# Seven products for eight (Strassen's scheme) in four of the eleven blocks of each down projection

## What is computed

```python
D_MODEL, SEQ, DEPTH = 1024, 256, 2
D_FF = 2816

def hybrid_layer(x, ...):
    h = rms_norm(x, g_attn_pre)
    ...                       # projection, two kinds of attention, w_out
    x = x + rms_norm(jnp.einsum('bse,ed->bsd', mix, w_out), g_attn_post)
    h = rms_norm(x, g_ffn_pre)
    f = jax.nn.silu(jnp.einsum('bsd,df->bsf', h, w_gate)) * jnp.einsum('bsd,df->bsf', h, w_up)
    x = x + rms_norm(jnp.einsum('bsf,fd->bsd', f, w_down), g_ffn_post)
    return x
```

## Time and profile before

| | |
|---|---|
| time, median of 3 runs | 571.66 us (571.55 to 571.73) |
| span of the profiled execution | 569.7 us |
| PE busy | 562.0 us (99%), 3395 matmuls |
| DVE busy | 375.1 us (66%) |
| ACT busy | 294.0 us (52%) |
| POOL busy | 229.1 us (40%) |

### The profile page before, as it was taken

One profiled execution on the slowest core, in us unless ns is written; L12 is line 12 of the kernel. 1 busy time (PEld: TensorE's weight loads), 2 busy tenths in 40 slices (PEclk: granted clock), 3 DMA queues, 4 the chain that ended last, 5 costly groups with the idle time before them and its releaser, 6 DMA issues.

```text
span 569.7 us, 8885 instructions
## 1 busy us (share of the span) xinstructions
PE 562.0 (99%) x3395; PEld 462.1 (81%) x3395; DVE 375.1 (66%) x487; ACT 294.0 (52%) x420; POOL 229.1 (40%) x451
## 2 busy tenths in 40 slices
PE   8999999999999999999999999999999999999996
PEld 5878878888888888888888878888888888888884
DVE  5799895946755746365597987775855746734622
ACT  6576684664445353263546748574645354425420
POOL 1101001507797797860120000033296797785000
PEclk9999999999999999999999999999999999999999
DMA  8954624538556461478266443525575455352701
GB/s 299 370 210 156 237 89 173 223 133 315 184 217 202 167 221 33 189 294 298 89 239 208 158 167 124 211 76 221 222 258 201 173 217 183 113 221 88 282 1 74
DMA packets 18730, 107.34 MB, mean 188 GB/s; under 512 B 2816, under 2 KB 3072, under 8 KB 7168
## 3 DMA queue, kind: packets, MB, share of 16 engines
q1 hardware_dynamic: 18688, 106.78, 50.8%
HBM read 105.72 MB, written 1.05 MB: 187 GB/s over the span
## 4 chain that ended last, share of the span: by engine, by line
PE 93%; DVE 3%; DMA 1%; ACT 1%; issue 1%; POOL 0%; SPq 0%; DVEq 0%; POOLq 0%
PE bank L1209 84%; PE bank L1249 4%; PE bank L1234 2%; PE bank L1275 2%; PE bank L1302 2%; DVE w_l L812 1%; DMA raw<-in_w_blocks 1%; ACT work L631 0%; DVE work L896 0%; DVE work L874 0%; DVE work L897 0%; DVE work L952 0%; DVE work L902 0%; DVE x L986 0%; ACT work L608 0%
## 5 line engine op out<-in xcount | busy, mean ns | idle before, releaser
L812 DVE TENSOR_TENSOR w_l<-raw,w_h 128x2048 fp32r<-128x2048 f32 x90 | 206.6, 2301 | 112.6 <-ACT w_h L559 112.4
L559 ACT ACTIVATE w_h<-raw 128x2048 fp32r<-128x2048 f32 x90 | 171.7, 1915 | 108.5 <-PE bank L1209 91.5
L1209 PE MATMUL bank<-w_h,actT_h 128*128 128x512 f32 (+1 forms) x568 | 223.9, 394 | 0.1
L517 POOL COPY work<-work 32x128 f32<-32x128 f32 (+1 forms) x384 | 191.3, 498 | 75.6 <-DVE work L1013 59.8
L1209 PE MATMUL bank<-w_h,actT_l 128*128 128x512 f32 (+1 forms) x568 | 219.9, 387 | 0.0
L1209 PE MATMUL bank<-w_l,actT_h 128*128 128x512 f32 (+1 forms) x568 | 219.4, 386 | 0.0
L1209 PEld LDWEIGHTS bank<-w_h,actT_h 128*128 128x128 f32 x568 | 106.8, 188 | 23.1 <-issue 2.5
L1209 PEld LDWEIGHTS bank<-w_h,actT_l 128*128 128x128 f32 x568 | 106.7, 188 | 22.1
L1209 PEld LDWEIGHTS bank<-w_l,actT_h 128*128 128x128 f32 x568 | 106.9, 188 | 20.1
L504 POOL TENSOR_TENSOR norms<-norms,constants 128x1 f32<-128x1 f32 x8 | 2.7, 342 | 131.7 <-ACT bank L658 131.7
L1209 PE MATMUL bank<-w_h,fT_h 128*128 128x512 f32 x160 | 49.4, 390 | 0.0
(11 more groups left out here) (78 smaller groups left out, 396.1 us busy)
## 6 DMA issues: line engine op xcount, KB each, us to landing
raw<-in_w_blocks SPq DMA_DIRECT2D x90, 1024.0 KB, 4.8
bias<-in_b_in SPq DMA_DIRECT2D x8, 256.0 KB, 6.1
raw<-in_w_blocks SPq DMA_DIRECT2D x4, 256.0 KB, 5.9
raw<-in_w_blocks SPq DMA_DIRECT2D x2, 512.0 KB, 8.6
x<-in_x SPq DMA_DIRECT2D x2, 512.0 KB, 10.7
gain_b<-in_g_attn_post SPq DMA_DIRECT2D x2, 512.0 KB, 7.3
bias<-in_g_ffn_pre SPq DMA_DIRECT2D x2, 512.0 KB, 7.4
gain_b<-in_g_ffn_post SPq DMA_DIRECT2D x2, 512.0 KB, 6.5
```

The lines of the kernel that those rows point to most:

```text
L517: ins = nc.gpsimd.tensor_copy(crossed[t][32 * j:32 * j + 32, i * n:(i + 1) * n], squares[t][32 * i:32 * i + 32, j * n:(j + 1) * n])
L559: nc.scalar.activation(w["h"][:, slot(b), :], raw[:, r, :], ACT.Copy).then_inc(hi_ready, 1)
L812: nc.vector.tensor_tensor(w["l"][:, slot(b), :], raw[:, slot(b, RAW), :], w["h"][:, slot(b), :].bitcast(F32), ALU.subtract).then_inc(lo_re ...
L1209: ins = nc.tensor.matmul(bank[BANK_OF[name]][:, 0:n], left[s][:, at + k, tokens(t)], right[r][:, k, c * BANK:c * BANK + n], start=first an ...
```

## The change

Four of the eleven down blocks of each layer are multiplied by Strassen's scheme in Winograd's form. Such a block holds 2 k; with 2 tiles of tokens and 2 halves of the columns it is a product of a 2x2 by a 2x2 matrix of squares. Instead of 8 products of squares (24 matmuls) PE does 7 (21 matmuls). The products use four sums of squares of f (S1 to S4) and four sums of squares of weights (T1 to T4).

- **Blocks.** A fast block is two entries of `BLOCKS`: "raw", the loaded squares (three of its four squares, 1536 columns, are split into high and low, 9 matmuls), and "sum", T1 to T4 (2048 columns, 12 matmuls), which is not loaded. The list is 35 down, 36 raw, 37 sum, 38 down, 39 raw, 40 sum, 41 down, 42 raw, 43 sum, 44 raw, 45 sum, then 46 to 49 down. The number of loads stays 46 a layer. Slots go round by four without a skip.
- **Sums of weights.** `add_squares(n)` on DVE: three `tensor_tensor` from SBUF to SBUF, of 1024, 512 and 512 elements on 128 partitions, each waiting for the one before. ACT's `hi` of a sum block waits for `sums_ready`. A raw block's place in `raw` is free only after its `lo` and its sums.
- **Sums of f.** In chunks 1 and 2 `add_s` on DVE (four `tensor_tensor` of 256 elements) makes S1 to S4 of chunks 0 and 1; `hi_s` on ACT and `lo_s` on DVE (1024 elements each) split them. `add_s` waits for both exchanges of the chunk and stands ahead of `lo_f` and `swiglu`. POOL's exchange waits for it.
- **Joining.** The first product M1 gathers in bank 4, M6, M5 and M7 in banks 5 to 7 over all four fast blocks. ACT copies M1 out (`keep_m1`); DVE adds the combinations to the four result banks (`join_first`, `join_second`, eight operations on 512 columns). PE waits for the joins (`joined`).
- **Order on PE at the end.** After the last fast block: half of block 46 for t = 1, then blocks 46 to 49 for t = 0, then the rest for t = 1.

The core of the diff:

```diff
-KF_OWN = 20
-BLOCKS += [("down", k, 2, 0, D) for k in range(0, KF, 2)]
+FAST = 4
+FAST_CHUNKS = FAST // 2
+RAW_AT = []
+for n in range(FAST):
+    if n < FAST - 1:
+        BLOCKS += [("down", 2 * (FAST + n), 2, 0, D)]
+    RAW_AT += [len(BLOCKS)]
+    BLOCKS += [("raw", 2 * n, 2, 0, D), ("sum", 2 * n, 2, 0, D)]
+FIRST_LATE = len(BLOCKS)
+BLOCKS += [("down", k, 2, 0, D) for k in range(4 * FAST - 2, KF, 2)]
...
+SUMS = 2
+def slot(L, b):
+    return (L * NB + b) % SLOTS
+def before(b):
+    return b - SLOTS
...
+        sums = [gains[:].rearrange("p (a n) -> p a n", a=2), work_row[:, 0:4 * BANK].rearrange("p (a n) -> p a n", a=2)]
+        m1_sum = rope_tmp
+        u4, u2, u3, u7 = (work[:, q, :] for q in (0, 2, 3, 2))
+        s_raw = work_row[:, 0:2 * BANK].rearrange("p (s k n) -> p s k n", s=4, k=2)
...
+                    past_L, past = divmod(load_count(L, b) - RAW, NL)
+                    place_free(lo_ready, past_L * NB + LOADED[past] + 1)
+                    if BLOCKS[LOADED[past]][0] == "raw":
+                        place_free(sums_ready, sums_done(past_L, BLOCKS[LOADED[past]][1] // 2))
...
+                if 0 < c <= FAST_CHUNKS:
+                    pool.wait_ge(s_added, FAST_CHUNKS * L + c)
...
+                if m == "sum":
+                    act.wait_ge(sums_ready, sums_done(L, k0 // 2))
...
+            def hi_s(L, c):
+                act.wait_ge(s_added, FAST_CHUNKS * L + c + 1)
+                nc.scalar.activation(s_tiles("h", c), s_raw.rearrange("p s k n -> p (s k) n"), ACT.Copy
+                                     ).then_inc(s_hi_ready, 1)
+            def keep_m1(L):
+                act.wait_ge(block_used, USED.done(L, FIRST_LATE - 2) + USED.n)
+                nc.scalar.activation(m1_sum, products[0][:], ACT.Copy).then_inc(m1_kept, 1)
...
+                        if c <= FAST_CHUNKS:
+                            hi_s(L, c - 1)
                         after(L, b + 3)
                 hi_f(L, FFN_CHUNKS - 2, 0)
+                after(L, FIRST_DOWN)
                 hi_f(L, FFN_CHUNKS - 2, 1)
-                for b in range(FIRST_DOWN, NB - 4):
+                for b in range(FIRST_DOWN + 1, NB - 4):
+                    if b == RAW_AT[FAST - 1]:
+                        keep_m1(L)
                     after(L, b)
-                    if b == FIRST_DOWN + 4:
+                    if b == RAW_AT[1]:
                         hi_f(L, FFN_CHUNKS - 1, 0)
                         hi_f(L, FFN_CHUNKS - 1, 1)
...
+            def add_s(L, c):
+                for t in range(T):
+                    dve.wait_ge(crossed_in[t], f_count(L, c))
+                if L or c:
+                    dve.wait_ge(s_lo_ready, FAST_CHUNKS * L + c)
+                s1, s3, s2, s4 = (s_raw[:, q].rearrange("p k (i b) -> p k i b", b=32) for q in range(4))
+                a11, a12 = f_odd(c, 0, 0), f_odd(c, 0, 1)
+                a21, a22 = f_odd(c, 1, 0), f_odd(c, 1, 1)
+                nc.vector.tensor_tensor(s3, a11, a21, ALU.subtract)
+                link(L, nc.vector.tensor_tensor(s1, a21, a22, ALU.add))
+                link(L, nc.vector.tensor_tensor(s2, s1, a11, ALU.subtract))
+                nc.vector.tensor_tensor(s4, a12, s2, ALU.subtract).then_inc(s_added, 1)
+            def lo_s(L, c):
+                dve.wait_ge(s_hi_ready, FAST_CHUNKS * L + c + 1)
+                nc.vector.tensor_tensor(s_tiles("l", c), s_raw.rearrange("p s k n -> p (s k) n"),
+                                        s_tiles("h", c).bitcast(F32), ALU.subtract).then_inc(s_lo_ready, 1)
...
+            def add_squares(L, n):
+                b = RAW_AT[n]
+                r = raw_slot(L, b)
+                dst = sums_of(n)
+                b12, b11, b22, b21 = (raw[:, r, q * BANK:(q + 1) * BANK] for q in range(4))
+                dve.wait_ge(raw_in[r], raw_done(L, b))
+                link(L, nc.vector.tensor_tensor(dst[:, 0, :].rearrange("p (a n) -> p a n", a=2),
+                                                raw[:, r, BANK:3 * BANK].rearrange("p (a n) -> p a n", a=2),
+                                                b12.unsqueeze(1).broadcast_to([P, 2, BANK]), ALU.subtract))
+                link(L, nc.vector.tensor_tensor(dst[:, 1, 0:BANK], dst[:, 0, BANK:2 * BANK], b11, ALU.add))
+                nc.vector.tensor_tensor(dst[:, 1, BANK:2 * BANK], b21, dst[:, 1, 0:BANK], ALU.subtract
+                                        ).then_inc(sums_ready, 1)
+            def join(L, t, c, what):
+                x = bank[BANK_OF["down", t, c]]
+                nc.vector.tensor_tensor(x[:], x[:], what, ALU.add).then_inc(joined, 1)
+            def join_first(L):
+                _, m6, m5, _ = products
+                dve.wait_ge(m1_kept, L + 1)
+                join(L, 0, 0, m1_sum)
+                dve.wait_ge(products_full, 3 * L + 1)
+                link(L, nc.vector.tensor_tensor(u2, m1_sum, m6[:], ALU.add))
+                dve.wait_ge(products_full, 3 * L + 2)
+                link(L, nc.vector.tensor_tensor(u4, u2, m5[:], ALU.subtract))
+                join(L, 0, 1, u4)
+            def join_second(L):
+                _, _, m5, m7 = products
+                dve.wait_ge(products_full, 3 * L + 3)
+                link(L, nc.vector.tensor_tensor(u3, u2, m7[:], ALU.add))
+                dve.wait_ge(second_begun, L + 1)
+                join(L, 1, 0, u3)
+                link(L, nc.vector.tensor_tensor(u7, u3, m5[:], ALU.subtract))
+                join(L, 1, 1, u7)
...
+                    if c == FFN_CHUNKS - 1:
+                        add_squares(L, 0)
                     after(L, b)
                     for q in range(b + 1, end):
                         after(L, q)
                     if c < FFN_CHUNKS - 1:
+                        if c <= FAST_CHUNKS:
+                            add_s(L, c - 1)
                         lo_f(L, c - 1, 0)
                         lo_f(L, c - 1, 1)
                     swiglu(L, c, 0)
                     after(L, end)
                     if c < FFN_CHUNKS - 1:
                         squares_f(L, c, 1)
-                for t in range(T):
-                    lo_f(L, FFN_CHUNKS - 2, t)
-                    squares_f(L, FFN_CHUNKS - 1, t)
-                for b in range(FIRST_DOWN, NB - 4):
-                    after(L, b)
-                    if b == FIRST_DOWN + 4:
-                        lo_f(L, FFN_CHUNKS - 1, 0)
-                        lo_f(L, FFN_CHUNKS - 1, 1)
+                    if c <= FAST_CHUNKS:
+                        lo_s(L, c - 1)
+                first, second, third, fourth = RAW_AT
+                add_squares(L, 1)
+                lo_f(L, FFN_CHUNKS - 2, 0)
+                squares_f(L, FFN_CHUNKS - 1, 0)
+                after(L, FIRST_DOWN)
+                lo_f(L, FFN_CHUNKS - 2, 1)
+                squares_f(L, FFN_CHUNKS - 1, 1)
+                after(L, first)
+                add_squares(L, 2)
+                after(L, first + 1)
+                after(L, first + 2)
+                after(L, second)
+                add_squares(L, 3)
+                lo_f(L, FFN_CHUNKS - 1, 0)
+                lo_f(L, FFN_CHUNKS - 1, 1)
+                after(L, second + 1)
+                after(L, second + 2)
+                after(L, third)
+                after(L, third + 1)
+                join_first(L)
+                after(L, fourth)
+                after(L, fourth + 1)
+                join_second(L)
...
+                pe.wait_ge(f_lo_ready, F_PARTS.done(L, (c, 1)))
+                pe.wait_ge(s_lo_ready, FAST_CHUNKS * L + c + 1)
+                pe.wait_ge(lo_ready, L * NB + b + 1)
+                product(m1, a11, b11, first, last)
+                product(x12, s4, b22, False, last)
+                product(x11, a12, b21, False, last).then_inc(block_used, 1)
+                USED.tick(b)
+                pe.wait_ge(lo_ready, L * NB + b + 2)
+                ends = [product(m6, s2, t2, first, last), product(m5, s1, t1, first, last),
+                        product(m7, s3, t3, first, last)]
+                if last:
+                    for ins in ends:
+                        ins.then_inc(products_full, 1)
+                product(x21, a22, t4, False, last).then_inc(block_used, 1)
+                USED.tick(b + 1)
...
+                f_landed(L, FFN_CHUNKS - 3, T - 1)
+                for n in range(FAST):
+                    if n < FAST - 1:
+                        multiply(L, 0, RAW_AT[n] - 1)
+                        multiply(L, 1, RAW_AT[n] - 1)
+                    squares(L, n)
+                multiply(L, 1, FIRST_LATE, (0,), asks=True).then_inc(second_begun, 1)
+                multiply(L, 0, FIRST_LATE, asks=False, apart=True)
+                f_landed(L, FFN_CHUNKS - 2, 0)
+                multiply(L, 0, FIRST_LATE + 1)
+                multiply(L, 0, FIRST_LATE + 2)
+                f_landed(L, FFN_CHUNKS - 1, 0)
+                multiply(L, 0, FIRST_LATE + 3)
+                pe.wait_ge(joined, 4 * L + 4)
```

(8 more changed lines are left out.)

189 lines of the change are left out of this document (120 added, 69 removed).

## The result

The changed kernel takes 598.18 us (median of 4 runs, 597.66 to 598.63), the kernel before 571.68 us beside it. The ratio is 1.0465, 95% interval 1.045 to 1.0479: slower, by 26.5 us. The forecast was 595.4 us. A few executions on record were far longer than the others of their kernel (627 us and more); no ratio here uses them.

A forecast was written before the change was run, and what follows sets the result against it. PE, busy 99% at 0.2267 us a matmul, was taken to bound the kernel. Stalls from late DVE and POOL work, less the matmuls saved, came to +12.9 + 10.9 = +23.7 us on 571.66: 595.4 us, range 582 to 604.

The forecast's parts named there:

- X: End of POOL's exchange of chunk 3: later by 3.8 us in each layer, through DVE's sums of f.
- PE's start of the down projection: PE begins at X + 13.15: 233.3 instead of 226.01, and 509.6 instead of 504.20.
- next layer's first blocks: Start of the next layer: its first blocks take their slots as early as before, so nothing is added.
- The first wait: Start of the down projection: PE waits for `swiglu(5, 0)` behind sums, `hi` 37 and `lo` 37; 7.3 and 5.4 us.
- The second wait: Later down blocks: PE waits 1.3 us for `lo` 41 and 4.5 us at block 44, whose `hi` stands behind POOL's copies.
- The joins: End of the down projection: PE waits for the first two joins, 1.15 + 0.9 us a layer.
- The clock falls: Rival: PE's pauses drop it to 1.2 GHz, delaying blocks 44 to 47 by 2 to 4 us a layer; 601 us, chance 0.13.
- Only the handover: Rival: the sums don't hold POOL up, or it catches up while PE stands; 583.0 us, chance 0.16.
- The gain shows: Rival: `swiglu(5, 0)` and every `lo` in time, only saved matmuls and joins count; 566.2, up to 570.3 us, chance 0.08.
- the 0.5 us of air: Before the first down matmul: `swiglu(5, 0)` ends 0.5 us before PE starts, and 2.7 us of sums go in there.

The follow-up runs named there:

- e9: The kernel before with three DVE operations of the weight sums' sizes, results unused, added ahead of `lo` 37: 573.75 us.
- e5: The changed kernel with the sums of weights cut to 8 elements per operation: 585.1 us.
- e6: The changed kernel with the sums of f cut to 8 elements and their low part to one column: 588.44 us.
- e8: The changed kernel with 26 matmuls of 512 columns added on PE ahead of each down projection, to keep it busy through the first wait: 598.11 us.
- e4: The changed kernel with the three additions of `add_squares` replaced by transposes of the same sizes, with one input: 587.99 us.
- e7: The changed kernel with both the sums of weights and the sums of f cut down: 574.47 us.
- e10: The changed kernel with the sums of weights, the sums of f and the joins all cut down: 572.4 us.
- v2: v1 with `keep_m1` and the joins moved ahead of chunk 5's `hi_f` and `lo_f`: 569.62 us, ratio 0.9965 to the kernel before.
- e1: The changed kernel with both Silu moved ahead of `hi` 37 on ACT and both `swiglu` of chunk 5 ahead of `add_squares(0)` on DVE: 598.73 us.
- v1: The changed kernel with two fast blocks instead of four, behind three plain ones, `swiglu(5, 0)` ahead of the last plain `lo`: 588.17 us.

## Why the prediction was right

It was right by its mechanism and its sum. Single terms were off, and part of the closeness of the sum is luck: one term was 3.0 us too small, and the waits behind the start were 1.1 us a layer too large.

| step | predicted, L0 / L1 | measured, L0 / L1 |
|---|---|---|
| X, end of chunk 3's exchange | +3.8 / +3.8 | +4.2 / +6.8 |
| PE's start of the down projection | +7.3 / +5.4 | +7.7 / +8.3 |
| waits and slow matmuls from there to the end of the down projection | 8.3 / 8.3 | 7.15 / 7.15 |
| next layer's first blocks | 0 | 1.05 |
| the layer's part of the loss | +12.9 / +10.9 | +13.4 / +12.8 |

(X is 201.30 + 19.30 and 493.45 + 19.35; the values of layer 1 are less the 13.38 us by which its feed-forward part begins later. The third line is the sum of all distances between matmuls less 0.2267 each. The forecast named 7.85 us of waits there; its own reckoning, from X + 13.15 to X + 69.0, holds 8.3. The fifth is of the profiled spans, 26.1 us together where 23.7 were forecast.)

**X in layer 1 is the term that was mis-sized.** I took POOL's delay as the same addition in both layers. But the kernel before ran in step with PE in layer 1 and not in layer 0, and the change puts both layers out of step, so layer 1 pays the 2 to 3 us that layer 0 had paid already. e9, which found layer 0 in step as well, shows that the course is no property of the layer. These 3.0 us are more than the forecast lacked in all (2.8 us); the waits behind the start, forecast 1.1 us a layer too long, take 2.3 us off again, and the 1.05 us at the next layer's first blocks, which it put at nothing, come on top.

**The first wait** is as described: sums, `hi` 37, `lo` 37, `swiglu(5, 0)`. e5 (6.12) and e6 (3.39) show what the sums of weights and those of f have in it, 2 and 4.7 us in layer 0; 3.5 us had been forecast for what stands without POOL's delay.

**The second wait** was forecast as 1.3 us at block 41 and 4.5 at block 44. The first is in e8 alone (0.93 us); in the changed kernel the slow matmuls ahead of it covered it. The second was 3.42 and 2.75, shorter because `lo` 44 came at X + 48.8 and not at 49.5 and PE came later. Its cause holds: ACT's row waits for POOL, and `hi` 44 stands behind it.

```profile
265.74 0.42 ACT L676 ACTIVATE actT_h<-work 128x256 fp32r<-128x256 f32 x1 [4.96 <-POOL work L590]
266.06 1.47 ACT L641 ACTIVATE w_h<-raw 128x1536 fp32r<-128x1536 f32 x1
```

X + 45.8 was 266.0 by the forecast; the row is at 265.74. In e4, where only the hold on POOL is taken away, this wait is gone. The Trainium skill (SBUF — State Buffer, "Who interferes with whom") gives the contention that the forecast named; e4 agrees for the sums, 41.72 us against 34.71.

**The joins** were forecast at 2.05 us a layer, and show 1.0 and 0.2. In layer 0 `join_first` began at X + 55.4 and not at 56.45; in layer 1 it was as early, and PE came later besides, by the slow matmuls behind the wait at block 44. e7 less e10 puts them at 2.1 us altogether where nothing else is in the way.

**The rivals.** "The clock falls" came half true. The forecast had the matmul stay at 0.2267 us; behind both first waits, and in layer 1 behind block 44 too, matmuls were 0.43 us apart. By e8 the fall after the first wait cost nothing, for the reason given there (PE waits again). The fall behind block 44 in layer 1 made matmuls 1.5 us longer. No run removes it alone, but the third line of the table is 7.15 us in layer 0, without this fall, and in layer 1, with it: what it cost was taken off the waits around it. The Trainium skill (TensorE: Matmul & The Clock Gate, Part 1) has it that an idle PE drops to 1.2 GHz, and the trace agrees after the pauses of 8 us (granted clock 0.76 in the window behind the first). "Only the handover" (583.0) fell with the wait at block 44. "The gain shows" (566.2) is not reached even with all sums and joins left out (572.4): the forecast named the 0.5 us of air as what stands against it, and that was too mild.

**What the forecast didn't ask** is whether the place of the fast blocks, and not the scheme, makes the loss. It took the sums' time as due at the handover, since there the diff puts them. v2 shows that half as much of this work is covered when three plain blocks stand ahead and nothing that PE wants soon is queued behind POOL. Whether the work for four fast blocks would be covered too was not tried.

## What to carry to other kernels

Work saved on the bounding engine is gained only if what replaces it on the other engines is due where they have slack: count, at the point of handover, how much work each queue has in front of what the bounding engine wants next, and put plain work there first. When a stall moves on reordering (e1), look at what the late engine itself waited for: there DVE waited for ACT and ACT for POOL. See that nothing due early stands in a queue behind something that comes late (v1 to v2, 18.6 us by order alone). Work added to a queue costs less where it fills a wait (e9) than where another engine's step has to come behind it (the changed kernel). A loop that runs in step with another engine has a cost of being put out of step, which an experiment on one profiled execution may miss.

## What the hardware showed that I had not expected

- A DVE operation with two inputs in SBUF holds POOL's copies up and a transpose of the same length, with one, hardly does: 64 copies take 41.72 us beside the sums, 34.71 beside transposes of 1.20, 0.71 and 0.71 us, 35.08 beside neither. The `tensor_tensor` with one input in PSUM doesn't hold them up either: 19 copies of 64 elements beside v2's joins, 0.27 us from one to the next.
- The clock after a pause is not the same each time. After 8.13 us the window read 0.76. After 3.42 us in layer 0 it stayed at 1.00, after 2.75 us in layer 1 it fell:

```profile
265.00:275.00 10.00, 6.58 (x28) 4.89 (x27) 7.82 (x5) 7.68 (x6) 0.62 (x3) 1.00 0.37 113
...
560.00:566.00 6.00, 4.37 (x13) 3.56 (x14) 5.96 (x4) 5.70 (x4) 0.00 (x0) 0.72 0.48 175
```

- The same loop may take another course: POOL's loop of the kernel before ran at 22.3 us from start to start in layer 0 and at 21.76 in layer 1, and in e9 at 21.76 in layer 0 too. e9's ten runs spread over 4.3 us, where the kernel before beside them kept within 0.6. That the runs of e9 differ by this course is likely but not shown, for only one of them was profiled.
